# Two heads' scores ahead of a projection, the next projection among the last heads, and outputs transposed chunk by chunk

## The reference

```
q, kv = rmsnorm(c_q) @ w_uq, rmsnorm(c_kv) @ w_ukv          # MLA: k and v of each head from kv
s = (q_nope @ k_nope^T + q_rope @ k_rope^T) * scale         # causal
o = softmax(s) @ v                                          # 16 heads of 64 -> 1024 columns
h = h + o @ w_o
# NSA: o = g0 * o_compressed + g1 * o_selected + g2 * o_window, then h + o @ w_o
# memory and window branch: y = softmax(q k^T * scale) v * silu(z), q and z being projections of h
```

## Time and profile before

| | us |
|---|---|
| median of 3 runs | 1556.27 |
| the profiled execution | 1556.23 |
| its span, first to last instruction | 1554.4 |
| PE busy | 1474.4 (95%) |
| DVE busy | 941.2 (61%) |
| ACT busy | 738.9 (48%) |

### The profile page before, as it was taken

How to read it: one execution, slowest core, us unless ns; L and a number is a source line. 1 busy time by engine, 2 the same in 40 slices (tenths; PEclk the granted TensorE clock), 3 DMA queues, 4 the chain that set the end, 5 groups by cost and what they waited for, 6 DMA issues and landing times.

```text
span 1554.4 us, 24190 instructions
## 1 busy us (share of the span) xinstructions
PE 1474.4 (95%) x9470; PEld 1351.2 (87%) x9470; DVE 941.2 (61%) x1344; ACT 738.9 (48%) x1004; POOL 46.0 (3%) x88
## 2 busy tenths in 40 slices
PE   7999978899989999989999999999998999999997
PEld 7899978899987888888998888788887999988886
DVE  4545686555556666648456666666666458766665
ACT  5546543243435454436445445544544428555444
POOL 1000000100000000010002000000000000000000
PEclk9999989999998999978589999999999999999999
DMA  8443420155543555524036555475554510355552
GB/s 304 136 155 109 163 82 28 57 203 188 184 149 116 208 182 195 198 94 163 1 109 223 204 194 170 159 249 194 179 195 157 190 55 2 109 186 180 197 194 95
DMA packets 33909, 239.13 MB, mean 154 GB/s; under 512 B 3946, under 2 KB 4090, under 8 KB 5808
## 3 DMA queue, kind: packets, MB, share of 16 engines
q1 hardware_dynamic: 32544, 232.02, 43.2%
q0 software_dynamic: 1296, 6.15, 1.2%
HBM read 237.07 MB, written 1.08 MB: 153 GB/s over the span
## 4 chain that ended last, share of the span: by engine, by line
PE 79%; DVE 3%; ACT 2%; issue 1%; POOL 0%; POOLq 0%; DVEq 0%; ACTq 0%
PE ps L669 20%; PE ps L640 12%; PE ps L641 12%; PE ps L642 12%; PE ps L672 10%; PE ps L771 3%; PE ps L794 2%; PE ps L781 1%; PE ps L999 1%; PE ps L2219 1%; PE ps L2211 1%; DVE low L380 1%; PE ps L582 1%; PE ps L2223 1%; PE ps L2337 1%
## 5 line engine op out<-in xcount | busy, mean ns | idle before, releaser
L380 DVE TENSOR_TENSOR low<-raw,high 128x2048 fp32r<-128x2048 f32 (+1 forms) x193 | 437.7, 2268 | 255.5 <-ACT high L374 254.9
L374 ACT ACTIVATE high<-raw 128x2048 fp32r<-128x2048 f32 (+1 forms) x193 | 364.3, 1888 | 65.2 <-PE ps L642 59.9
L669 PE MATMUL ps<-nt,high 128*128 128x512 f32 x1344 | 335.8, 392 | 0.0
L669 PEld LDWEIGHTS ps<-nt,high 128*128 128x128 f32 x1344 | 244.2, 189 | 46.3 <-issue 0.9
L640 PE MATMUL ps<-nt,high 128*128 128x256 f32 x736 | 213.8, 290 | 5.7 <-DVE nt L471 4.7
L641 PE MATMUL ps<-nt,high 128*128 128x256 f32 x736 | 212.0, 288 | 0.0
L642 PE MATMUL ps<-nt,low 128*128 128x256 f32 x736 | 211.9, 288 | 0.0
L672 PEld LDWEIGHTS ps<-nt,low 128*128 128x128 f32 x1344 | 183.3, 190 | 13.1
L672 PE MATMUL ps<-nt,low 128*128 128x256 f32 x1344 | 187.4, 282 | 0.0
L640 PEld LDWEIGHTS ps<-nt,high 128*128 128x128 f32 x736 | 145.4, 198 | 7.3 <-DVE low L380 4.2
L641 PEld LDWEIGHTS ps<-nt,high 128*128 128x128 f32 x736 | 145.5, 198 | 0.0
(11 more groups left out here) (343 smaller groups left out, 2233.4 us busy)
## 6 DMA issues: line engine op xcount, KB each, us to landing
raw<-in_stream SPq DMA_DIRECT2D x217, 1024.0 KB, 4.8
late<-in_w POOLq DMA_DIRECT2D x1, 2048.0 KB, 8.5
scr<-bias_by_distance POOLq DMA_DIRECT2D x1, 2048.0 KB, 12.8
scr<-in_mem SPq DMA_DIRECT2D x2, 512.0 KB, 4.9
x<-in_x SPq DMA_DIRECT2D x1, 1024.0 KB, 8.7
out<-xs SPq DMA_DIRECT2D x2, 512.0 KB, 2.6
row<-in_row SPq DMA_DIRECT2D x1, 588.0 KB, 10.5
con<-in_con SPq DMA_DIRECT2D x1, 577.0 KB, 9.6
```

The source lines that it names most:

```text
L374: nc.scalar.activation(high[t % SLOTS][:, 0:n], raw[t % SLOTS][:, 0:n], ACT.Copy).then_inc(w_high, 1)
L380: nc.vector.tensor_tensor(low[t % SLOTS][:, 0:n], raw[t % SLOTS][:, 0:n], high[t % SLOTS][:, 0:n].bitcast(F32), ALU.subtract).then_inc(w_l ...
L669: nc.tensor.matmul(r3(bank, 2), wt[0][:, k, col:col + P], nt[:, :, k, :], start=k == 0, stop=False, skip_group_check=True)
```

## The change

Five edits, all of them a matter of order:

1. `lead`: in all four stages PE computes the scores of the first two heads first, and then a projection that stood ahead of the attention: `xmz1`, `swz1`, the second half of `uv`, or `nvw`. ACT and DVE make the steps that belong to it (reading the bank, splitting a later weight tile) at the same place, ahead of their work for the third head.
2. `ready`: where the projection makes values, PE waits for them just ahead of the first product with the values.
3. `fill`: in XM and SW the next projection (`swq0`, `gmv0`) is cut in two halves (`pe_half`), put before the transposes and the values of the last heads. The next one follows whole, then the transposes of y, so that their splits on ACT and DVE come after the steps of two projections.
4. `y`: in MLA and in the second half of NSA the transposes of y are put into the iterations, one chunk of 128 columns every two heads, into the banks 4 and 5 (the last quarter into bank 0). Their splits on ACT and DVE (`act_y`, `dve_y`) follow every four heads.
5. `pe_y_out`: the first output projection works on the chunks that are ready while the last head is finished.

The value projection of MLA also changes its banks: 2 and 3 for the first two parts, 4 and 5 for the others. Shortened to its core:

```diff
+        def pe_half(pe, name, kind, j):
+            t, out_ = TILE[name], ps[bank_of(name)]
+            if j == 0:
+                weights_here(pe, t)
+                pe.wait_ge(bank_done[UNIT[name] % 2], plain_free(name))
+            if kind == "F":
+                last = by_feature(out_[:, S * j:S * j + S], slot(t, KC, CW), P * j, NT_, KC)
+            else:
+                last = by_token(out_[:, CW * j:CW * j + CW], slot(t, KC, CW), 0, CW, NT_, KC, j)
+            if j:
+                last.then_inc(w_used, 1)
...
+        Y_OUT = {"mly": "mlao0", "nsy": "nsao0"}
+        def y_bank(name, b):
+            out_bank = bank_of(Y_OUT[name])
+            return ps[(9 - out_bank, out_bank, 9 - out_bank, 0)[b]]
+        def y_turned(name, b):
+            return turn_at[name] + b + 1
+        def pe_y(pe, name, c):
...
+            src, b = TURNS[name][0], c // 2
+            if c == 4:
+                pe.wait_ge(turn_low, y_turned(name, 0))
+            for t in range(TT):
+                at = 256 * (c % 2) + P * t
+                last = nc.tensor.transpose(y_bank(name, b)[:, at:at + P], src[:, t, P * c:P * c + P], ident)
+            if c % 2:
+                last.then_inc(turned, 1)
+        def act_y(act, name, b):
+            act.wait_ge(turned, y_turned(name, b))
+            nc.scalar.activation(TURNS[name][3][:, 2 * b:2 * b + 2, :], r3(y_bank(name, b), 2), ACT.Copy)\
+                .then_inc(turn_high, 1)
+        def dve_y(dve, name, b):
+            dve.wait_ge(turn_high, y_turned(name, b))
+            nc.vector.tensor_tensor(TURNS[name][4][:, 2 * b:2 * b + 2, :], r3(y_bank(name, b), 2),
+                                    TURNS[name][3][:, 2 * b:2 * b + 2, :].bitcast(F32), ALU.subtract)\
+                .then_inc(turn_low, 1)
...
+        def pe_y_out(pe, y, first):
+            name = Y_OUT[y]
+            t, out_, acts = TILE[name], ps[bank_of(name)], TURNS[y][3:5]
+            w = slot(t, KC, CW)
+            weights_here(pe, t)
+            pe.wait_ge(bank_done[UNIT[name] % 2], plain_free(name))
+            pe.wait_ge(turn_low, y_turned(y, 1))
+            def part(j, ks):
+                for k in ks:
+                    if k % 2 == 0:
+                        pe.wait_ge(turn_low, y_turned(y, k // 2))
+                    last = split_product(out_[:, CW * j:CW * j + CW], [a[:, k, P * j:P * j + P] for a in acts],
+                                         [v[:, k, :] for v in w], j + k == 0, k == KC - 1)
+                return last
+            part(0, range(4))
+            pe.wait_ge(at_read, first)
+            pe_y(pe, y, KC - 1)
+            part(0, range(4, 6))
+            part(1, range(6))
+            part(0, range(6, KC))
+            part(1, range(6, KC)).then_inc(w_used, 1)
...
+        def pe_units(pe, first, n, lead, ready, fill=None, y=None):
...
             for a in range(first, first + n + 3):
+                if a == first + 2:
+                    lead()
                 if a < first + n:
                     scores(a)
+                if fill and a == first + n + 1:
+                    fill(0)
                 if first <= a - 2 < first + n:
                     turn_probs(a - 2)
+                if fill and a == first + n + 2:
+                    fill(1)
+                if a == first + 3:
+                    ready()
                 if first <= a - 3:
                     values(a - 3)
+                c, odd = divmod(a - (first + n - 2 * KC) - 6, 2)
+                if y and odd == 0 and c >= 0:
+                    pe.wait_ge(at_read, first + n - 2 * KC + 2 * c + 2)
+                    pe_y(pe, y, c)
...
-        def act_units(act, first, n, sinks=False):
+        def act_units(act, first, n, lead, sinks=False, y=None):
             for a in range(first, first + n + 2):
+                if a == first + 2:
+                    lead()
...
+                b, off = divmod(a - (first + n - 2 * KC) - 9, 4)
+                if y and off == 0 and b >= 0:
+                    act_y(act, y, b)
...
+        def dve_units(dve, ch, first, n, evac, lead, sinks=False, y=None):
             for a in range(first, first + n + 4):
+                if a == first + 2:
+                    lead()
...
+                b, off = divmod(a - (first + n - 2 * KC) - 10, 4)
+                if y and off == 0 and b >= 0:
+                    dve_y(dve, y, b)
...
+            act_z("xmz0", xm["z"])
+            act_units(act, XM0, XM_H, lambda: act_z("xmz1", xm["z"]))
...
-                                                     r3(read_bank(act, name), TT), ACT.Silu))
...
+            act_turn(act, "ym")
+            act_z("swz0", sw["z"])
+            act_units(act, SW0, SW_H, lambda: act_z("swz1", sw["z"]), sinks=True)
...
-            act_step(act, "uv")
-            act.wait_ge(w_used, TILE["uv"] + 1)
-            for t in range(TT):
-                nc.scalar.activation(as3(ml["v"], TT)[:, t, 0:512], ps[2 * t][:, :], ACT.Copy).then_inc(ml_va, 1)
-            act_units(act, MLA0, MLA_H)
-            act_turn(act, "mly")
+            act.wait_ge(ml_v, 1)
+            nc.scalar.activation(as3(ml["v"], TT)[:, 0, 0:512], ps[2][:, :], ACT.Copy).then_inc(ml_va, 1)
+            def act_v():
+                act_step(act, "uv")
+                act.wait_ge(ml_v, 3)
+                nc.scalar.activation(as3(ml["v"], TT)[:, 1, 0:512], ps[4][:, :], ACT.Copy).then_inc(ml_va, 1)
+            act_units(act, MLA0, MLA_H, act_v, y="mly")
             act_added(act, "f1", [f"mlao{j}" for j in range(4)])
             act_ffn(act, 1, "f2")
...
-            bank_read("nvw", nc.scalar.activation(ns["vw"], read_bank(act, "nvw")[:, :], ACT.Copy))
-            act_units(act, NSA0, 2 * NSA_H)
-            act_step(act, "nvw")
-            act_turn(act, "nsy")
+            def act_vw():
+                bank_read("nvw", nc.scalar.activation(ns["vw"], read_bank(act, "nvw")[:, :], ACT.Copy))
+                act_step(act, "nvw")
+            act_units(act, NSA0, 2 * NSA_H, act_vw, y="nsy")
...
+            def dve_z(names):
+                dve_step(dve, names[1])
+                for name in names:
+                    wait_bank(dve, name)
...
+            dve_step(dve, "gmv0")
+            dve_step(dve, "gmv1")
             dve_turn(dve, "yc")
-            for name in ("gmv0", "gmv1", "gmu0"):
-                dve_step(dve, name)
+            dve_step(dve, "gmu0")
...
                 nc.vector.tensor_copy(mk_[0:64, 4 * b + 1:4 * b + 4:2, :], r3(ps[4 + b][64:128, :], 2))\
                     .then_inc(ml_kd, 1)
-            dve_step(dve, "uv")
-            dve.wait_ge(w_used, TILE["uv"] + 1)
-            for t in range(TT):
-                nc.vector.tensor_copy(as3(ml["v"], TT)[:, t, 512:1024], ps[2 * t + 1][:, :]).then_inc(ml_vd, 1)
-            dve_units(dve, ch, MLA0, MLA_H, attention_evac(as3(ml["y"], TT), MLA0, MLA_V))
-            dve_turn(dve, "mly")
+            dve.wait_ge(ml_v, 2)
+            nc.vector.tensor_copy(as3(ml["v"], TT)[:, 0, 512:1024], ps[3][:, :]).then_inc(ml_vd, 1)
+            def dve_v():
+                dve_step(dve, "uv")
...
-            dve_units(dve, ch, NSA0, 2 * NSA_H, nsa_evac)
-            dve_step(dve, "nvw")
-            dve_turn(dve, "nsy")
+            dve_units(dve, ch, NSA0, 2 * NSA_H, nsa_evac, lambda: dve_step(dve, "nvw"), y="nsy")
...
-            for name, kind in (("xmq1", "F"), ("xmz0", "T"), ("xmz1", "T")):
-                pe_plain(pe, name, kind)
+            pe_plain(pe, "xmq1", "F")
+            pe_plain(pe, "xmz0", "T")
             for name in ("mk0", "mk1", "mv0", "mv1", "xmq0", "xmq1"):
                 wait_bank(pe, name)
-            pe_units(pe, XM0, XM_H)
+            def nothing():
+                pass
+            pe_units(pe, XM0, XM_H, lambda: pe_plain(pe, "xmz1", "T"), nothing,
+                     lambda j: pe_half(pe, "swq0", "F", j))
+            pe_plain(pe, "swq1", "F")
             pe.wait_ge(at_read, XM0 + XM_H)
             pe_turn(pe, "ym")
-            for name, kind in (("swq0", "F"), ("swq1", "F"), ("swkv", "FT"), ("swz0", "T"), ("swz1", "T")):
...
-            pe.wait_ge(ml_vd, 2)
+            def v_part(n, bank):
+                return by_token(bank[:, :], slot(TILE["uv"], 2, D), 512 * (n % 2), 512, NT_, 2, n // 2, 3)
+            v_part(0, ps[2]).then_inc(ml_v, 1)
+            v_part(1, ps[3]).then_inc(ml_v, 1)
             pe.wait_ge(ml_ka, 4)
             pe.wait_ge(ml_kd, 4)
             pe.wait_ge(ml_krd, 1)
-            pe_units(pe, MLA0, MLA_H)
-            pe.wait_ge(at_read, MLA0 + MLA_H)
-            pe_turn(pe, "mly")
-            for j in range(4):
-                pe_plain(pe, f"mlao{j}", "T", None if j else "mly", NTY)
-                if j:
-                    pe_late_turn_both(pe, "f1", j - 1)
+            def rest_of_v():
+                v_part(2, ps[4]).then_inc(ml_v, 1)
+                v_part(3, ps[5]).then_inc(w_used, 1)
+                pe.wait_ge(ml_va, 1)
+                pe.wait_ge(ml_vd, 1)
```

(59 more changed lines are left out.)

39 lines of the change are left out of this document (20 added, 19 removed).

## The result

The changed kernel takes 1534.93 us (median of 4 runs, 1534.46 to 1534.99) against 1556.06 for the kernel before in the same measurement (4 runs, 1555.51 to 1556.74): ratio 0.9863, 95% interval 0.9846 to 0.988. Beside these executions it is 21 us faster; 4 were forecast.

What follows compares the result with a forecast made beforehand. PE was bounded by waiting and by working at 1.2 GHz. From 1554.4, -4.2 - 1.6 + 1.6 - 2.6 gave 1547.6, or 1551.0 with a short NSA fall; adding 1.8, 1549.4 and 1552.8; taken 1552, range 1526 to 1584.

Steps and rivals of the forecast that it cites:

- XM and SW: Memory and sliding-window attention: reordered scores and projections fill PE idle of 2.5 and 2.1 us; net -4.2 us.
- The waits of 0.8 and 0.6: New PE waits before the third head's transposes in memory and sliding-window attention, with the table load back to Exp.
- the overlap term: In memory and sliding-window attention, six fewer idle ends, each costing 0.16 us of lost matmul overlap: 1.0 us.
- MLA's entry: PE waits 2.5 us at one place, for the second half of the values; clock fall taken at 5 in 8.
- MLA's heads: With the clock low from about 737, sixth head's scores end earlier, later heads unchanged: -1.6 us, bounds -2.8 and +1.
- then 3.20 per head as before: After the sixth head's scores in MLA, every head still takes 3.20 us at low clock.
- rival B: NSA's clock falls at its entry and stays down: 46 us more, 1595, or 1573 with MLA at full clock; chance 0.29.
- C: Clock falls in NSA's last 16 heads, where the transposes of y are now: 24 us, 1576; chance 0.04.
- the slow rivals: NSA's clock staying low from its entry, or falling in its last 16 heads; slower, together 0.33.
- NSA: Entry waits of 1.1, 2.2 and 0.3 us cost +1.6, exit -2.6, a short clock fall +3.4.
- A: MLA at full clock, its entry wait causing no fall: -24.4 us instead of -1.6, 1529; chance 0.25.
- the likeliest case: The forecast itself: 1552 us, MLA's clock low, NSA without a fall or with a short one; chance 0.42.

Runs made afterwards that it cites:

- the kernel with late splits: The changed kernel with MLA's and NSA's moved weight split on ACT and DVE placed after the last head instead of ahead of the third; 1519.7 to 1520.6 us.

## Why the prediction was right and wrong

**XM and SW (-4.2 forecast, -3.5 measured).** The waits of 0.8 and 0.6 were 0.82 and 0.76. What was wrong is a last wait of SW's values, which stayed (0.58 us, before 0.47): PE's idle fell from 4.6 to 2.2 us, by 2.4 and not by 3.2. The rest, 1.0 us, is as large as the overlap term, but only three of six places fell away, worth 0.5; what the other 0.5 is remains open.

**MLA's entry.** Wait 2.5 forecast, 2.27 measured, for the reason given; the clock fell, as I took with 5 in 8.

**MLA's heads (-1.6 forecast, -18.7 measured): the step that failed** is "then 3.20 per head as before". Up to there it held: the sixth head's scores came 1.5 us earlier, for 1.6. Two heads then took 3.20 us each and the third, with the first pair in it, 3.63; from the ninth head's scores on they ran at full clock. I had weighed the transposes of y for the time that they add and took 0. They gave 14 to 20 us (1549.2 to 1555.4 without them; 13.9 by the two traces at MLA's exit), by bringing the clock back; with one pair in the kernel before no execution lies above 1540.0. Why a pair does it is argued only: it adds full-row work to heads whose scores use 96 rows. The rows for this stood in the prediction: 96 against 128 rows was named under rival B, and 3.68 us of y transposes ahead of the rise at 787.7 under C. I used both against the slow rivals and not for this step.

**NSA (+2.4 forecast with a short fall, +0.7 measured).** Waits 0.95 and 1.80 for 1.1 and 2.2, so the entry cost 1.2 for 1.6; exit -2.2 for -2.6; the fall lasted 3.4 us for the 6.8 taken, 1.7 us less.

**The rivals.** A (1529) came nearest in time by another way: the clock did fall. B (1595) came only when I put NSA's scores on 96 rows: NSA then stayed low for 61 us. C did not happen; the rise, not a fall, stands behind the transposes. So the rule that I set beside C does not hold here: the Trainium skill, "TensorE: Matmul & The Clock Gate", section "Part 4: PE-mode transpose", says transposes do not count as busy in the same way, and here a pair of transposes and a pair of matmuls brought the clock back alike (1538.1 to 1539.4 and 1539.2 to 1540.0 us).

**The kernel before.** I read its long low stretch as fixed. It is one of two courses; 43 of 81 executions did not take it. The range (1526 to 1584) held the result, the likeliest case (1546 to 1557) did not. That it lies in the range is luck: A's 1529 had widened the range for an execution without a fall, and the result came with the fall, by a mechanism that the prediction had priced at 0. That the change is faster at all holds beside executions of 1556 us; beside those of 1531 it is 0.26% slower.

What the better order alone is worth is seen where the clock plays little part: by the starts of the same matmuls, the kernel with late splits against the kernel before in its execution of 1530 us is ahead by 2.7 us ahead of MLA, 6.4 behind it and 10.2 behind NSA (1.7 of which is the short fall at MLA's entry). The changed kernel, in its second profile and set against the same execution, is 2.5 ahead before MLA, 2.1 behind after it and 3.3 behind after NSA: it gives 13 us back by its own waits and the low clock behind them.

## What to carry to other kernels

Read the granted clock of each stage before its busy share, and ask two things of it: which wait stands ahead of the fall, and what PE does behind it. Here a fall was cheap where scores on all 128 rows followed (3.4 or 6.8 us) and dear behind scores on 96 (54.6 us). There one pair of full tiles among the heads took 17 to 18 us off the executions of 1556 us, and four matmuls of constants in the wait 25; the better order by itself is worth 10. Take profiles of several executions, too: one alone showed only one of two courses. A step that is moved brings its weight split along: behind the last head it cost 0.51 us, in the ramp it cost waits of 2.27 and 2.75 and two falls of the clock.

## What the runs showed of the hardware

- At 1.2 GHz and with PE 99 to 100% busy the clock stayed low for 41.0 us (scores on 96 rows, in MLA without the pairs) and 61.4 us (the same in NSA), and came back 3.4 or 6.8 us after its fall in NSA with scores on 128 rows.
- The rise stood 1.5 to 3.0 us behind the start of a single pair of 128x128 transposes (0.63 us) in three kernels' profiles, and 1.5 us behind that of a pair of plain matmuls (1.17 us) in a fourth.
- A PE wait of 2.15 or 2.16 us at MLA's entry was followed by a fall in every profile that has it (five); with matmuls of constants in it there was none.
- Executions of the same program differ by 26 us on the same chip; 23 of them lie in MLA, by the length of one low stretch (3.4 or 54.6 us).
- The table load back from Silu to Exp (1.28 us) stands ahead of the exponentials for which PE waits 0.82 us in XM and 0.76 in SW.
